# A fused two-block transformer kernel: the two norms of block two start on the unnormed residual

## What is computed

```python
mod = c_act @ w_mod[l] + b_mod[l]
sh1, sc1, g1, sh2, sc2, g2 = [m[:, None, :] for m in jnp.split(mod, 6, axis=-1)]

h = rmsnorm_2(x, attn_norm_g[l]) * (1.0 + sc1) + sh1
proj = jnp.einsum('bsd,df->bsf', h, w_in[l])
...
x = x + g1 * jnp.einsum('bsm,md->bsd', mix, w_out[l])

h = rmsnorm_2(x, mlp_norm_g[l]) * (1.0 + sc2) + sh2
u = jax.nn.relu(jnp.einsum('bsd,df->bsf', h, w_ff1[l]))
x = x + g2 * jnp.einsum('bsf,fd->bsd', u * u, w_ff2[l])
```

## Time and profile before

| What | Value |
|---|---|
| median of three runs | 2135.23 us |
| the profiled execution's own time | 2135.95 us |
| its span from first to last instruction | 2134.1 us |
| PE busy | 2110.7 us, 99% |
| DVE busy | 1485.1 us, 70% |
| ACT busy | 1057.9 us, 50% |
| POOL busy | 36.1 us, 2% |
| DMA | 496.80 MB, mean 233 GB/s |

### The profile page before, as it was taken

How to read it: one execution, slowest core, us unless ns; L and a number is a source line. 1 busy time by engine, 2 the same in 40 slices (tenths; PEclk the granted TensorE clock), 3 DMA queues, 4 the chain that set the end, 5 groups by cost and what they waited for, 6 DMA issues and landing times.

```text
span 2134.1 us, 29149 instructions
## 1 busy us (share of the span) xinstructions
PE 2110.7 (99%) x11394; PEld 1826.2 (86%) x11394; DVE 1485.1 (70%) x1973; ACT 1057.9 (50%) x1515; POOL 36.1 (2%) x40
## 2 busy tenths in 40 slices
PE   9999999999999999999999999999999999999998
PEld 7888888888888888888888898888888888888886
DVE  6867665788989888899756666576555565555655
ACT  6654555554444434444455665555443444344443
POOL 1200000000000000000000000000000000000000
PEclk9999999999999999999999999999999999999999
DMA  8786333788888988888854524555555555555553
GB/s 346 259 310 241 119 103 126 279 308 321 341 333 321 363 325 327 323 338 335 300 188 153 209 91 168 178 184 195 194 197 194 186 192 193 188 191 198 183 185 126
DMA packets 73207, 496.80 MB, mean 233 GB/s; under 512 B 8410, under 2 KB 8618, under 8 KB 16496
## 3 DMA queue, kind: packets, MB, share of 16 engines
q1 hardware_dynamic: 69984, 481.85, 63.0%
q0 software_dynamic: 2512, 12.44, 1.5%
q10 hardware_dynamic: 576, 0.66, 0.1%
HBM read 492.75 MB, written 2.16 MB: 232 GB/s over the span
## 4 chain that ended last, share of the span: by engine, by line
PE 94%; ACT 2%; DVE 2%; issue 1%; DMA 0%; POOL 0%; DVEq 0%; ACTq 0%; SPq 0%
PE region L1013 41%; PE region L957 30%; PE region L961 15%; PE bank L1082 2%; PE bank L1045 2%; PE region L1002 1%; PE bank L1054 1%; ACT m_WHI L1350 1%; PE region L1003 1%; PE bank L996 1%; PE bank L1095 0%; ACT m_HL L1535 0%; POOL m_Z L2020 0%; DVE m_WLO L1693 0%; PE bank L1170 0%
## 5 line engine op out<-in xcount | busy, mean ns | idle before, releaser
L1693 DVE TENSOR_TENSOR m_WLO<-m_RAW,m_WHI 128x1024 fp32r<-128x1024 f32 (+3 forms) x732 | 878.6, 1213 | 519.6 <-ACT m_WHI L1350 503.5
L1350 ACT ACTIVATE m_WHI<-m_RAW 128x1024 fp32r<-128x1024 f32 (+3 forms) x732 | 756.3, 1043 | 710.9 <-PE region L1013 387.2
L1013 PE MATMUL region<-m_WHI,m_HL 128*128 128x512 f32 x1152 | 361.4, 395 | 1.1 <-issue 0.6
L957 PE MATMUL region<-m_HL,m_WHI 128*128 128x512 f32 x1472 | 358.3, 393 | 0.0
L957 PE MATMUL region<-m_H,m_WHI 128*128 128x512 f32 x1376 | 328.7, 391 | 0.0
L957 PEld LDWEIGHTS region<-m_HL,m_WHI 128*128 128x128 f32 x1472 | 270.0, 189 | 52.0
L957 PEld LDWEIGHTS region<-m_H,m_WHI 128*128 128x128 f32 x1376 | 252.8, 188 | 48.9
L1013 PEld LDWEIGHTS region<-m_WHI,m_HL 128*128 128x128 f32 x1152 | 212.8, 188 | 43.6 <-issue 1.4
L1729 DVE CUSTOM_DVE_ANT_0 m_RAW<-m_RAW,m_CROW,m_consts 128x2048 f32<-128x2048 f32 x96 | 225.6, 2350 | 0.4 <-issue 0.4
L1013 PE MATMUL region<-m_WLO,m_HL 128*128 128x512 f32 x576 | 224.6, 390 | 0.0
L1013 PE MATMUL region<-m_WHI,m_HIDH 128*128 128x512 f32 x512 | 199.2, 389 | 0.0
(11 more groups left out here) (300 smaller groups left out, 1777.9 us busy)
## 6 DMA issues: line engine op xcount, KB each, us to landing
m_RAW<-in_w_ff SPq DMA_DIRECT2D x124, 1024.0 KB, 4.9
m_RAW<-in_w_mod SPq DMA_DIRECT2D x96, 1024.0 KB, 6.0
m_RAW<-in_ffn_w_in SPq DMA_DIRECT2D x88, 1024.0 KB, 6.5
m_RAW<-in_ffn_w_out SPq DMA_DIRECT2D x44, 1024.0 KB, 5.1
m_RAW<-in_nsa_w_in SPq DMA_DIRECT2D x36, 1024.0 KB, 5.6
m_RAW<-in_nsa_w_out SPq DMA_DIRECT2D x16, 1024.0 KB, 4.8
m_RAW<-in_w_out SPq DMA_DIRECT2D x16, 1024.0 KB, 4.9
m_RAW<-in_w_in SPq DMA_DIRECT2D x8, 1024.0 KB, 6.7
```

What stands on the lines that cost most here:

```text
L957: mm = e.matmul(region[s["reg"]][:, b, :], hi[:, i, c:c + 128], both[:, k + a + i, :, :].rearrange("p a s -> p (a s)"), start=k + a + i == ...
L1013: mm = e.matmul(o, lhs, rhs, start=start and i == 0, stop=fin and i == 2, skip_group_check=True)
L1350: e.activation(WHI[u % 4][:, 0:(z - a) * ncol], raw[:, a * ncol:z * ncol], ACT.Copy).then_inc(a_hi, 1)
L1693: e.tensor_tensor(WLO[u % 4][:, 0:m], raw[:, a * ncol:z * ncol], WHI[u % 4][:, 0:m].bitcast(F32), ALU.subtract).then_inc(v_lo, 1)
```

## The change

The two slabs behind each norm no longer read normed tiles. They read XGT split into HI and LO (tiles u4 and u6, unit `usplit`, two tiles a unit), which has the norm's gain but neither root nor shift. As the root is one number per token, and the shift gives one number per output column, both are put on the result: qa 0 and 1 get them in `qfix` (DVE multiplies by the root, ACT adds `shifted`), relu 0 and 1 in `ufix`, then `urelu`. `shifted` holds eight columns, each a sum of the shift times a column of the weight. They are made by eight loads of 1 MB and eight DVE passes (`shiftsum`), behind the 96 of `gemv` in the same queue, and by two small stores and two row loads on POOL's queue (`shift`, `shiftrow`). The dealing rate goes from 0.75 to 0.8 for each chunk.

The slabs in front of the norms run whole, no longer by halves, and the matmuls of ones are gone. The split is always four parts ahead of PE. The normed tiles are made four at a time, for ka (or relu 2) and all later slabs. `hook` puts each unit of the seam behind one named k-tile of one named slab. The diff, cut to its core:

```diff
-        s = dict(tail={("down1z", 12): 1, ("out2", 12): 1, ("down2z", 12): 2}.get((kind, arg), 0), i=len(self.slabs), kind=kind, arg=arg, w=w, row0=row0, kts=kts, c0=c0, nc=ncol,
+        s = dict(tail=2 if (kind, arg) == ("down2z", 12) else 0, i=len(self.slabs), kind=kind, arg=arg, w=w, row0=row0, kts=kts, c0=c0, nc=ncol,
...
-    sl_qa = [slab("qa", i, W, 0, KT, 256 * i, 256, WIDE, "h4", per=4) for i in range(2)]
+    sl_qa = [slab("qa", i, W, 0, KT, 256 * i, 256, WIDE, "u4", per=4) for i in range(2)]
...
-        up = [slab("relu", j, "w_ff1_2", 0, KT, 256 * (s0 + j), 256, WIDE, "h6", per=4 if s0 + j < 2 else None)
+        up = [slab("relu", j, "w_ff1_2", 0, KT, 256 * (s0 + j), 256, WIDE, "u6" if s0 + j < 2 else "h6",
+                   per=4 if s0 + j < 2 else None)
...
-    gemvs = deque((p, j) for p in range(6) for j in range(16))
+    gemvs = deque(("g", (p, j)) for p in range(6) for j in range(16))
+    for r in range(2):
+        gemvs.extend([("row", r), None] + [("s", 4 * r + i) for i in range(4)])
...
+        what, i = g
+        if what == "row":
+            put("shiftrow", i)
+            return
+        load(what, i)
+        if what == "s":
+            put("shiftsum", i)
+            return
+        p, j = i
         put("gemv", p, j)
-        if j == 15 and p in (1, 4):
-            put("factors", p // 4)
-        if j == 15 and p in (2, 5):
-            put("gate", p)
-
-    def ahead(s, k):
-
-        if s["arg"] >= 2:
-            return KT
-        step = k // 4 * 2 + s["arg"]
-        if step < 2:
-            return (4 + k, 8 + k // 2)[step]
-        return 11 + (step - 2) * 2 + (k % 4 >= 2)
+        if j == 15:
+            put({0: "shift", 1: "factors", 2: "gate"}[p % 3], p // 3)
...
+    def make_u(x, m):
+        assert have[x] == m
+        put("usplit", x, m)
+        have[x] = m + 2
+
+    def make_norm(x):
+        put("norm", x, normed[x])
+        normed[x] += 1
+
+    def hook(s, kx, f, *a):
+        hooks.setdefault((s["i"], kx), []).append((f, a))
...
-            while normed[x] < min(KT, ahead(s, k)):
-                put("norm", x, normed[x])
-                normed[x] += 1
-                if normed[x] == 2:
-                    put("rowkeep", 2 if x == "h4" else 3)
-                if normed[x] == 9:
-                    put("turnout", x, 12)
-        elif x in ("h2", "h3", "h5"):
+            while normed[x] <= k // 4:
+                make_norm(x)
...
+    def late_norm(x, last, one, two, three):
+
+        r = 2 if x == "h4" else 3
+        for m in range(0, 12, 2):
+            hook(last, m + 5, make_u, "u" + x[1], m)
+        hook(two, 0, put, "stat", r)
+        hook(two, 1, unit, "xturn", x, 12)
+        hook(one, 6, make_u, "u" + x[1], 12)
+        hook(one, 6, make_u, "u" + x[1], 14)
+        hook(one, 7, unit, "rowcast", r)
+        hook(two, 5, make_norm, x)
+        hook(one, 9, make_norm, x)
+        hook(one, 14, make_norm, x)
+        hook(three, 1, make_norm, x)
+        if x == "h4":
+            for s, kx, m0 in ((two, 6, 0), (two, 9, 4), (two, 13, 8), (three, 4, 12)):
+                hook(s, kx, put, "final", m0)
+            hook(three, 7, put, "qfix", 0)
+            hook(three, 9, put, "qfix", 1)
         else:
-            put("sqhalf", 2 if s["kind"] == "out2" else 3, s["arg"], h)
-
-    def idle(n):
-
-        put("ones", n, P.bank_count[7])
-
-    def finish_by_halves(s):
-
-        which = {"down1z": "h4", "out2": "h6", "down2z": None}[s["kind"]]
-        row_half(s, 0)
-        if which is None:
-            put("stat4", 0)
-            put("store", 0)
-        for j, (n, kk) in enumerate(st["held"]):
-            put("mm2", n, kk)
-            if which and j == 2:
-                P.uses(("xturn", which, 12), 4, 5)
-                put("turnhalf", which, 12, 0)
-        st["held"].clear()
-        row_half(s, 1)
-        if which is None:
-            put("stat4", 1)
-            put("store", 1)
-            return
-        idle(5)
-        put("turnhalf", which, 12, 1)
-        put("stat", 2 if which == "h4" else 3)
-        idle(6)
-        unit("rowcast", 2 if which == "h4" else 3)
-        idle(6)
-        st["owed"] = 2
+            for s, kx in ((one, 5), (two, 7)):
+                hook(three, kx, put, "ufix", s["i"])
+                hook(three, kx + 4, put, "urelu", s["i"])
+                hook(three, kx + 4, put, "hid", s["i"])
...
-            side.extend([None] * 3 + [("xturn", "h4", m0)])
+            if m0 < 12:
+                side.extend([None] * 3 + [("xturn", "h4", m0)])
         elif kind == "out2":
             put("sumsq", 2, m0)
-            side.extend([None] * 6 + [("xturn", "h6", m0)])
+            if m0 < 12:
+                side.extend([None] * 6 + [("xturn", "h6", m0)])
...
-            if st["owed"] and kk % 2 == 0 and s["arg"] == 1:
-                st["owed"] -= 1
...
-    st["gemv"] = 0.75
+    st["gemv"] = 0.8
     run(out1[2], out1[3])
+    late_norm("h4", ffn1[1][1][3], sl_qa[0], sl_qa[1], sl_ka)
+    late_norm("h6", out2[3], *ffn2[0][0][0:3])
...
+            elif x in ("u4", "u6"):
+                w.wait_ge(a_u, kx // 2 + (1 if x == "u4" else 9))
+                w.wait_ge(v_u, kx // 2 + (1 if x == "u4" else 9))
+                xh, xl = HI[:, kx, :], LO[:, kx, :]
...
-            elif name == "ones":
-                n, turn_of_bank = arg
-                w.wait_ge(b_out[7], turn_of_bank)
-                for _ in range(n):
-                    e.matmul(bank[7][:, 0:128], ones[:, :], ones[:, :], start=True, stop=True)
...
+            elif name == "usplit":
+                x, m = arg
+                w.wait_ge(b_out[4 + m % 4 // 2], filled(("xturn", "h" + x[1], m // 4 * 4), 4 + m % 4 // 2))
+                w.wait_ge(p_part, tiles_free(x, m))
+                e.activation(HI[:, m:m + 2, :], XGT[:, m:m + 2, :], ACT.Copy).then_inc(a_u, 1)
...
+            elif name == "qfix":
+                i, = arg
+                w.wait_ge(v_qfix, i + 1)
+                w.wait_ge(v_shift, 4)
+                for t in range(2):
+                    m = 2 * i + t
+                    ins = e.activation(qaT[:, m, :], qaT[:, m, :], ACT.Identity, bias=shifted[:, m:m + 1])
+                ins.then_inc(a_qfix, 1)
...
-                x, m = arg
-                w.wait_ge(v_ht, product_no(x, m))
-                w.wait_ge(p_part, P.ffn1_end if x == "h4" else P.out2_end)
-                sh = mod[:, m:m + 1] if x == "h4" else mod[:, 48 + m:49 + m]
-                e.activation(HI[:, m, :], HT[m % 8 // 4][:, m % 4, :], ACT.Identity, bias=sh).then_inc(a_norm, 1)
+                x, c = arg
+                w.wait_ge(v_ht, c + (1 if x == "h4" else 5))
+                w.wait_ge(p_part, tiles_used(x, c))
+                for i in range(4):
+                    m = 4 * c + i
+                    sh = mod[:, m:m + 1] if x == "h4" else mod[:, 48 + m:49 + m]
+                    e.activation(HI[:, m, :], HT[c % 2][:, i, :], ACT.Identity, bias=sh).then_inc(a_norm, 1)
             elif name == "warm":
...
+                if s["x"] == "u6":
+                    return
...
+            elif name == "usplit":
+                x, m = arg
+                w.wait_ge(a_u, m // 2 + (1 if x == "u4" else 9))
+                e.tensor_tensor(LO[:, m:m + 2, :], XGT[:, m:m + 2, :], HI[:, m:m + 2, :].bitcast(F32), ALU.subtract).then_inc(v_u, 1)
+            elif name == "qfix":
+                i, = arg
+                dst = qaT[:, 2 * i:2 * i + 2, :]
+                w.wait_ge(*freed("qa", i))
+                w.wait_ge(b_out[6], filled(("rowcast", 2), 6))
...
+            elif name == "shiftsum":
+                i, = arg
+                raw, landing, value = raw_of("s", i)
+                w.wait_ge(landing, value)
+                w.wait_ge(l_shiftrow, 16 * (i // 4 + 1))
+                e.tensor_tensor_reduce(out=raw[:, :], in0=raw[:, :], in1=CROW[:, :], scale=0.125 if i < 4 else 1.0, scalar=0.0,
+                                       op0=ALU.mult, op1=ALU.add, accum_out=shifted[:, i:i + 1]).then_inc(v_shift, 1)
...
+                x, c = arg
+                base, sh, r = (0, 0, 2) if x == "h4" else (16, 48, 3)
+                w.wait_ge(b_out[6], filled(("rowcast", r), 6))
+                for b in (4, 5):
+                    w.wait_ge(b_out[b], filled(("xturn", x, 4 * c), b))
+                if c < 2:
                     w.wait_ge(a_hid, 22)
                     w.wait_ge(v_hidlo, 22)
+                    if x == "h6":
+                        w.wait_ge(p_values, 32)
                 else:
+                    w.wait_ge(a_norm, base + 4 * c - 4)
+                    w.wait_ge(v_norm, base + 4 * c - 4)
+                e.tensor_tensor(HT[c % 2][:, :, :], XGT[:, 4 * c:4 * c + 4, :], by_token(rstd, 4), ALU.mult).then_inc(v_ht, 1)
+                for i in range(4):
+                    m = 4 * c + i
+                    w.wait_ge(a_norm, base + m + 1)
```

(54 more changed lines are left out.)

109 lines of the change are left out of this document (56 added, 53 removed).

## The result

The changed kernel takes 2141.95 us (median, 2139.47 to 2143.68) against 2135.38 us for the kernel before in the same comparison (2133.83 to 2135.7): ratio 1.0031, 95% interval 1.0023 to 1.0040. It is 0.3% slower. The profiled execution's own time is 2141.94 us, its span 2140.0.

The account below looks back on a forecast made before the run. PE, busy 99% of the span, was taken as the bound. Seam terms +2.5 and -0.7 plus 3.4 for the clock gave +5.2 on 2135.95, so 2141.2; less 0.7, a median of 2140.4 us, range 2127 to 2147.

Parts of the forecast that it names:

- The removal: At both norm seams, 6.0 and 5.5 us between last slab and first tile go; 12.5 us less if nothing else waited.
- T: End of the last slab before each norm seam, forecast 0.4 us earlier: 1157.5 at h4 and 1414.1 at h6.
- The chain: In-order ACT and DVE work up to qa 0's read-out: ka 2.5 us later, relu 2 0.7 us sooner.
- all three engines are nearly full: Behind a norm, PE busy 23.15 and 22.99 us; ACT 21.49 of 24.19 us and DVE 21.18.
- the first rival: Norm seams: ACT and DVE work overlaps and PE's early start is kept, 2122.7 us fully, 2129 half; chance 0.20.
- Behind ka's and relu 2's start the chain needs less than PE: After the seams: norm 3 comes out near T + 40, and PE wants it at T + 41.5.
- `qfix` and `ufix` at nothing: In ka and relu 2, these units cost nothing because ACT and DVE have half their time free there.
- The clock: PE idles 8.0 us at h4 and 5.2 at h6, its clock falls: 1.7 us a seam, 3.4 in all.
- 4.6 us after PE stopped: Behind the kernel's last matmul, the earlier trace's delay before the granted clock went to half.
- The second rival: Norm seams: the chain holds but the clock doesn't fall, or falls once: 2137.0 or 2138.7 us; chance 0.12.
- Dealing at nothing: Block one: eight more loads and sums at rate 0.8 cost nothing, hidden by splits four parts ahead; ends 0 and 5 us.
- The third rival: Block one: DVE at 92% falls behind for a few chunks, 5 us on top, 2145.4 us; chance 0.08.

Follow-up runs that it names:

- x2: Changed kernel with norm unit 2 moved from ahead of the first slab's read-out to behind it: 2142.77 us, ratio 1.0037 to the kernel before.
- x6: Changed kernel with DVE's product taken out of each norm unit and queued one split earlier: 2132.33 us, ratio 0.9986 to the kernel before.
- x7: x6 with last transposes and root queued earlier, read-out ahead of the third norm unit, `final` moved: 2123.97 us, ratio 0.9951 to the kernel before.
- x5: Changed kernel with both pauses filled by matmuls of ones, 36 at h4 and 23 at h6: 2140.29 us, ratio 1.0025 to the kernel before.
- x8: Changed kernel with only the h4 pause filled, by 36 matmuls of ones: 2141.11 us, ratio 1.0032 to the kernel before.
- x9: Changed kernel with only the h6 pause filled, by 23 matmuls of ones: 2140.64 us, ratio 1.0027 to the kernel before.
- x12: Changed kernel with both `qfix` units moved out of ka into qa 2, pauses not filled: 2141.19 us, ratio 1.0033 to the kernel before.
- x1: Changed kernel with 25 matmuls of ones in front of ka and 12 in front of relu 2: 2140.78 us, ratio 1.0028 to the kernel before.
- x4: Kernel before the change with its 17 matmuls of ones at each seam left out: 2136.05 us, ratio 1.0007 to the kernel before.

## Why the prediction was right, and where it wasn't

Forecast 2140.4, measured 2141.95, inside the range. By its own steps:

- **The removal.** Right: qa 0 and relu 0 begin at once. T was to come 0.4 earlier at each seam. It came 0.33 later at h4, since the up slabs had taken 0.71 longer and the start 0.06 (0.33 - 0.77 = -0.44).
- **The chain.** Right in mechanism and size. Forecast: ka at T + 33.1; measured 1191.26 - 1158.20 = 33.06. The first three products 6.4 and 7.4 us apart; measured 6.4 and 7.3. ka's wait 8.0; measured 8.4. Norm 3 out at T + 40; measured 40.3. relu 2: forecast T + 29.0, measured 29.5. One reading was too wide: "all three engines are nearly full" holds at h4, but at h6 ACT had 17.22 of 23.76 us. The 0.5 is a place in the queue that I didn't see: a `usplit` of 0.68 us on DVE stands ahead of the additions behind out2 12. x2 and x6 confirm that it is this order, and x7 that with another the early start is kept: 2123.97, beside the 2122.7 of the first rival, which needs a different order and not the same one overlapping.
- **"Behind ka's and relu 2's start the chain needs less than PE", and `qfix` and `ufix` at nothing.** Wrong. The chain goes on to ka's read-out, forecast at T + 46 and measured at T + 49.8 (1207.95 - 1158.20), and through relu 2. ACT's 2.43, 0.72 and 1.90 us in front of norm 3 and the two `qfix` are in it. x5, x8 and x9 show it as waits of 1.63 and 0.72 us as soon as the clock doesn't cover it.
- **The clock.** That it falls at both seams was right. Its price was not a term of the sum: I took 3.4 us, the matmuls are slowed by about that much (1.9 and 1.5), and the distances D4 and D6 give back 0.04 and 0.13 when it stays up, and at h6 0.9 and 1.3 against x12 and x8. The sum came out only because the chain behind ka's start, which I had at nothing, is as long. Right number, wrong term, and so luck. The 1.7 a seam had a weak source too: the clock's column shows 1.00 over the twenty matmuls of the earlier trace rows, so no row shows that it was the clock that slowed them.
- **"4.6 us after PE stopped"**, from the earlier trace rows, as what a pause needs. Not a bound: 2.84 us in x1 and three of 1.5 to 1.7 with bursts between them in x4 were enough, and in after itself the clock fell 2.4 and 2.0 us after PE stopped. The second rival rested on it and fell.
- **Dealing at nothing.** 0.71 us in the profile of after, and from 0 to 4.4 in others. The third rival's mechanism is real, and its chance of 0.08 was too low for a small price and about right for the full one. The DMA share and DVE's share forecast there were right; that 0.02 more of each changes nothing was not.

The miss in the profiled time, 2141.94 against 2141.2, is 0.7, the size of the dealing's: the seams' own misses, -0.44 and +0.45, cancel. The rest of the 1.5 in the median comes from taking off 0.7, because the profiled execution of before lay above its median, while that of after lies at its own. Why the executions of after spread over 4.2 us isn't shown; block one, the kernel's start and h6 all vary in the profiles.

What stays open is this: 0.3 us of the 1.5 that x9 gains at relu 2 and loses again have no wait in the trace, and how often block one loses a microsecond or more at rate 0.8 can't be told from ten profiles.

## What to carry to other kernels

Where PE is nearly full and its two helpers are at 72 to 90% in the same stretch, as behind the norms here, an earlier start for PE is worth what the helpers' queues allow: write down both in-order queues to the next read-out, and count a hand-over each time that one engine's step waits for the other. Put a producer's step (here the product by the root) one unit ahead in the list before anything is removed: that alone was worth 9.6 us here, and it turned a loss of 6.6 us into a gain of 2.8. Before a slow clock or a wait is put into a sum, ask what lies beside it, and take away both together as well as each alone. The slow clock cost 0.04 us beside a chain of its length, and 1.6 in x2, where nothing covered it.
